# Attention output of one key group per matmul, and the projection weights loaded in two halves

## What is computed

```python
# 8 query heads of 64, 2 key/value heads: group g serves heads 4g .. 4g+3
qc = q.reshape(bsz, nc, CHUNK, N_KV_HEADS, rep, HEAD_DIM)          # nc = 4 chunks of 64 tokens, rep = 4
scores = jnp.einsum('bcqgrd,bckgd->bgrcqk', qc, kb) * (HEAD_DIM ** -0.5)   # kb: the chunk before and its own, 128 keys
probs = jax.nn.softmax(jnp.concatenate([scores, sink], axis=-1), axis=-1)[..., :WINDOW]
out = jnp.einsum('bgrcqk,bckgd->bcqgrd', probs, vb)
y_attn = out.reshape(bsz, s, ATTN_WIDTH) @ w_attn_o[l]              # 512 rows: head 4g+t, dim d -> row g*256 + t*64 + d
mixed = gate_a * y_attn + gate_c * y_conv + gate_s * y_ssm
```

## Time and profile before

| | us |
|---|---|
| median of 3 runs (951.61 to 953.21) | 951.86 |
| the profiled execution, its own time | 953.21 |
| its span, first to last instruction | 951.4 |
| PE busy, of the span | 909.5 |
| DVE busy | 709.5 |
| ACT busy | 480.5 |

### The profile page before, as it was taken

How to read it: one execution, slowest core, us unless ns; L and a number is a source line. 1 busy time by engine, 2 the same in 40 slices (tenths; PEclk the granted TensorE clock), 3 DMA queues, 4 the chain that set the end, 5 groups by cost and what they waited for, 6 DMA issues and landing times.

```text
span 951.4 us, 15656 instructions
## 1 busy us (share of the span) xinstructions
PE 909.5 (96%) x6575; PEld 767.0 (81%) x6575; DVE 709.5 (75%) x940; ACT 480.5 (51%) x600; POOL 19.9 (2%) x14
## 2 busy tenths in 40 slices
PE   5799999999999999999999999999999999999996
PEld 2598986767677989989997999777777888888885
DVE  3773998999667677866678487999967775666666
ACT  4574347732745566546336324684374544343434
POOL 2200000000000000000000000000000000000001
PEclk9899999999999999999999999999999999999998
DMA  8974365646886647876793924354878545655631
GB/s 355 253 229 135 134 210 189 232 136 253 288 284 210 238 150 242 311 250 221 243 328 96 266 90 134 133 163 147 290 265 313 195 157 190 207 177 181 199 107 45
DMA packets 128565, 196.10 MB, mean 206 GB/s; under 512 B 30729, under 2 KB 90641, under 8 KB 122351
## 3 DMA queue, kind: packets, MB, share of 16 engines
q1 hardware_dynamic: 126119, 194.89, 61.3%
q10 hardware_dynamic: 2376, 0.21, 0.2%
HBM read 194.02 MB, written 1.06 MB: 205 GB/s over the span
## 4 chain that ended last, share of the span: by engine, by line
PE 69%; DVE 19%; DMA 5%; issue 3%; ACT 2%; SPq 1%; POOL 1%; ACTq 0%; DVEq 0%
PE bank L614 16%; PE bank L616 15%; PE bank L615 15%; PE bank L980 8%; DVE wlo L1554 5%; DVE yc L1849 5%; PE bank L981 4%; DMA raw<-in_w_mod 3%; PE bank L652 2%; PE bank L718 2%; PE bank L847 1%; DMA uc<-in_ssm_c_im 1%; PE bank L900 1%; PE bank L742 1%; POOL uc L1132 1%
## 5 line engine op out<-in xcount | busy, mean ns | idle before, releaser
L1554 DVE TENSOR_TENSOR wlo<-raw,whi 128x2048 fp32r<-128x2048 f32 (+1 forms) x135 | 302.5, 2242 | 169.6 <-PE bank L616 86.0
L1171 ACT ACTIVATE whi<-raw 128x2048 fp32r<-128x2048 f32 x132 | 251.0, 1909 | 124.8 <-DMA raw<-in_w_in 57.3
L614 PE MATMUL bank<-hb,whi 128*128 128x256 f32 x592 | 170.9, 289 | 4.0 <-DVE wlo L1554 4.0
L616 PE MATMUL bank<-hb,wlo 128*128 128x256 f32 x592 | 168.1, 284 | 0.0
L615 PE MATMUL bank<-hb,whi 128*128 128x256 f32 x592 | 168.1, 284 | 0.0
L614 PE MATMUL bank<-whi,bhi 128*128 128x512 f32 x304 | 121.6, 400 | 2.1 <-DVE blo L1948 1.1
L614 PEld LDWEIGHTS bank<-hb,whi 128*128 128x128 f32 x592 | 114.1, 193 | 6.8 <-DVE wlo L1554 4.6
L980 PE MATMUL bank<-hb,whi 128*128 128x512 f32 x336 | 119.0, 398 | 0.0
L616 PE MATMUL bank<-whi,blo 128*128 128x512 f32 x304 | 118.7, 391 | 0.0
L615 PE MATMUL bank<-wlo,bhi 128*128 128x512 f32 x304 | 118.7, 390 | 0.0
L615 PEld LDWEIGHTS bank<-hb,whi 128*128 128x128 f32 x592 | 114.1, 193 | 0.4
(11 more groups left out here) (276 smaller groups left out, 1133.1 us busy)
## 6 DMA issues: line engine op xcount, KB each, us to landing
raw<-in_w_mod SPq DMA_DIRECT2D x48, 1024.0 KB, 6.2
raw<-in_w_ffn_in SPq DMA_DIRECT2D x44, 1024.0 KB, 5.1
raw<-in_w_in SPq DMA_DIRECT2D x38, 1024.0 KB, 6.9
raw<-in_w_ffn_out SPq DMA_DIRECT2D x22, 1024.0 KB, 5.0
raw<-in_w_out SPq DMA_DIRECT2D x8, 1024.0 KB, 7.6
raw<-in_w_in SPq DMA_DIRECT2D x16, 256.0 KB, 4.6
raw<-in_ssm_glu_b SPq DMA_DIRECT2D x4, 1024.0 KB, 6.2
raw<-in_ssm_glu_a SPq DMA_DIRECT2D x4, 1024.0 KB, 5.3
```

Of the source, the lines that this page charges most:

```text
L614: mm(o, w_hi, a_hi, start=start, stop=False, skip_group_check=True)
L616: return mm(o, w_lo, a_hi, start=False, stop=stop, skip_group_check=True)
L1171: fn(whi[mi % N_HI][:, :], raw[SLOT[item]][:, :], ACT.Copy).then_inc(s_hi, 1)
L1554: part = V.tensor_tensor(wlo[mi % N_LO][:, n], raw[SLOT[("main", *divmod(mi, NB))]][:, n], whi[mi % N_HI][:, n].bitcast(F32), ALU.subtract)
```

## The change

Each round of `attend` now puts its four heads side by side in the columns, on the 64 output partitions that belong to its key group: one matmul of 512 columns where two of 256 columns stood (j = 0), and two of 256 columns where four of 128 stood (j = 1). The copy `att_copy` covers 64 partitions by 512 columns, where it covered 128 by 256. `att[:, t, :]` then holds heads t and 4+t, so the rows of `w_attn_o` have to lie in that order too: each `ao` block is loaded by two transfers of 512 KB, one for each half of the partitions, and `N_LOADS` tells the wait that two transfers make one block. All other steps keep their places.

```diff
@@ -178,7 +178,7 @@
-N_LOADS = {"q": 4}
+N_LOADS = {"q": 4, "ao": 2}
...
@@ -537,8 +537,12 @@
-                if kind in ("ao", "cp", "gla", "glb"):
-                    w = A[{"ao": "w_attn_o", "cp": "conv_pw_w", "gla": "ssm_glu_a", "glb": "ssm_glu_b"}[kind]]
+                if kind == "ao":
+
+                    w = A["w_attn_o"][l].rearrange("(g t d) n -> g d t n", g=NKV, d=HEAD)
+                    return [(k4[g * HEAD:(g + 1) * HEAD], w[g][:, :, n * 512:(n + 1) * 512]) for g in range(NKV)]
+                if kind in ("cp", "gla", "glb"):
+                    w = A[{"cp": "conv_pw_w", "gla": "ssm_glu_a", "glb": "ssm_glu_b"}[kind]]
...
@@ -800,15 +804,13 @@
                 pe.wait_ge(pt_copied, n + 1)
-                for odd in range(2):
-                    o = b_t[odd * HEAD:(odd + 1) * HEAD, 0:2 * P].rearrange("p (t q) -> p t q", t=2)
-                    probs = pT[:, odd:4:2, :]
-                    if j == 0:
-                        last = mm(o, vv[:, 0, p], probs, start=True, stop=True, skip_group_check=True)
-                    else:
-                        for c in range(2):
-                            last = mm(o[:, :, c * CHUNK:(c + 1) * CHUNK], vv[:, 1 + c, p], probs[:, :, c * CHUNK:(c + 1) * CHUNK],
-                                      start=(c == 0), stop=(c == 1), skip_group_check=True)
+                o = b_t[p, :].rearrange("p (t q) -> p t q", t=4)
+                if j == 0:
+                    last = mm(o, vv[:, 0, p], pT[:, :, :], start=True, stop=True)
+                else:
+                    for c in range(2):
+                        last = mm(o[:, :, c * CHUNK:(c + 1) * CHUNK], vv[:, 1 + c, p], pT[:, :, c * CHUNK:(c + 1) * CHUNK],
+                                  start=(c == 0), stop=(c == 1), skip_group_check=True)
                 last.then_inc(pv_ready, 1)
...
@@ -1324,8 +1326,9 @@
                 j, g = divmod(r, 2)
+                p = slice(g * HEAD, (g + 1) * HEAD)
                 act.wait_ge(pv_ready, 4 * l + r + 1)
-                fn(att[:, 2 * g:2 * g + 2, j * P:(j + 1) * P], b_t[:, 0:2 * P].rearrange("p (t q) -> p t q", t=2), ACT.Copy).then_inc(at_copied, 1)
+                fn(att[p, :, j * P:(j + 1) * P], b_t[p, :].rearrange("p (t q) -> p t q", t=4), ACT.Copy).then_inc(at_copied, 1)
```

## The result

The changed kernel takes **954.09 us** (median of 20 runs, 947.47 to 956.98) against 948.00 us of the kernel before (20 runs, 942.70 to 953.21). The ratio is 1.0056, with a 95% interval of 1.0036 to 1.0077: it is slower by 0.6%. The profiled execution took 956.22 us with a span of 954.3; that of before had 953.21 and 951.4.

What follows compares the result with a forecast made beforehand. PE was taken as the bound (busy 909.5 of 951.4 us), nearly tied with DVE in layer 1's attention. Layer 0's 1.66 plus layer 1's 1.45, 3.1 us, on a median of 951.86 gave 955.0, range 953.1 to 957.2.

Steps and rivals of the forecast that it cites:

- The matmuls: Rounds of `attend` on PE: 0.42 us more for j = 0 and 0.41 for j = 1, old matmuls having overlapped.
- the rival without a price on PE: Rounds of `attend`: side-by-side streams share the feed at half rate, so new rounds cost the same; 952.1 us, chance 0.07.
- The Trainium skill's lower speed-up for tiles: Rounds of `attend`: by 2.38x for three tiles, an estimated 1.59x for two, round 0.92 us, whole sum 2.6 us.
- ACT's copy: `att_copy` on ACT: +0.21 us for each of eight, covered by idle time except ahead of scaling L1306 in layer 1.
- Layer 0: Layer 0's attention: four rounds before 189.2 us on a PE without idle time, paid in full, +1.66 us.
- Layer 1's attention: Layer 1's attention: 0.21 from the copy in the first round, then 0.42 and 2 x 0.41, +1.45 us.
- the rival in which layer 1 absorbs it: Layer 1: DVE's and ACT's chain hides PE's slip after the first round, paying only 0.21; 953.7 us, chance 0.14.
- The half loads: `ao` loads in two halves: 0.4 us delay from one more issue, costing nothing at layer 1's `mod` load.
- The bounds of 0 and 2.6: Delay of the `ao` half loads in us, bounded from quarter loads taken as 64 partitions; 2.6 would cost 0.6.
- the rival of late half loads: Layer 1's `mod` matmuls wait 3.1 us more because half-rate halves stretch the queue by 5.1; 958.1 us, chance 0.07.
- The room: Layer 1's `mod` load, landing 677.9, needed by PE at 678.46: 0.56 us to spare, 2.0 with PE 1.45 late.
- The base: Starting time of the kernel before: 951.86 us, the median of the runs shown, to which 3.1 us was added.

Runs made afterwards that it cites:

- that half alone: New attend and copy in layer 0 only, loads as before, against the kernel before: 950.63 us, ratio 1.0002; by group +1.3 and +1.7 us.
- the padded kernel: The changed kernel with 24 tiny unused transposes added on TensorE, making its program as long as before: 953.96 us, ratio 1.0081 against the kernel before.

## Why the prediction was right, and where not

The sign, the range and the place were right: slower, 954.09 in 953.1 to 957.2. The forecast of 955.0 was 0.9 us off, but that is luck, for two errors of 3 to 4 us stand against each other in it: the base stood 3.86 us too high, and the difference between the medians was 6.09, not 3.1. Of these 6.09, 4.35 to 4.95 is the change. The rest comes from the split: before has ten runs in each group and its median between them, the changed kernel nine and eleven.

- **The matmuls, right.** 0.42 and 0.41 a round were forecast, 0.42 and 0.42 measured, from L652 as the row with the same column count. That two streams on separate output columns had really run side by side, and that one alone isn't faster, was the step on which the sign hung; the rival without a price on PE is out.
- **The Trainium skill's lower speed-up for tiles, not borne out.** By its 2.38x for three tiles, in "TensorE: Matmul & The Clock Gate", section "Measured speedup vs the span model", the new round would have taken an estimated 0.92 us; it took 1.00. For two tiles of this shape the factor here is 1.00 / 0.58 = 1.7.
- **ACT's copy, right.** 0.21 forecast, 0.20 measured, paid once in layer 1.
- **Layer 0, right.** 1.66 forecast, 1.66 or 1.67 in every trace with the new matmuls, 1.3 and 1.7 in the times of that half alone.
- **Layer 1's attention, right.** 1.45 forecast, 1.43 to 1.49 measured, with the first round at 0.2: the rival in which layer 1 absorbs it is out.
- **The half loads, wrong, twice in the same direction.** The first wrong term was the delay: 0.4 us taken from one more issue, where 2.0 to 2.4 was measured (7.2 to 7.3 us for both halves instead of 4.9 to 5.2). The bounds of 0 and 2.6 held by luck, because the quarter loads of the earlier trace rows, from which the 2.6 comes, were misread. They don't go into 64 partitions: the kernel writes `k8[:, :, ...]`, all 128 partitions and 64 columns of each, and their packets are of 256 bytes (0.73 MB in 2879), where those of the half loads are of 2 KB. The DMA view of before over 513 to 516 us:

```profile
DMA packets 2879, 0.73 MB, mean 243 GB/s; under 512 B 2879, under 2 KB 2879, under 8 KB 2879
```

So they said nothing of 64 partitions, neither as a bound nor against the rival of late half loads, and no row of before did. The Trainium skill, "SBUF — State Buffer", section "Door 1", had given the right size, an estimate of 2.4 us.
- **The room, the more serious error.** The prediction gave the `mod` load 0.56 us of room, "and 2.0 with PE 1.45 late". But this load may be issued only when `lo` of `ao` 0 has freed its buffer, and that `lo` slips with PE as well. The load's issue and PE's need of it move together, so the room stays where it was: in every trace the need comes 12.4 to 12.5 us after `ao` 1's issue and the `mod` load's issue 5.37 us after it. With 0.56 and the bound of 2.6 the price would have been 2.0, not 0.6. Measured: 1.5.
- **The rival of late half loads** named the right place and the right sign (a wait of PE for `raw<-in_w_mod` behind 678), with a chance of 0.07 and a price of 3.1 from the same false room. It came true at half its size, 1.5 us beyond the other terms.
- **The base.** 951.86 was the median of three runs that all lay in the upper group; over 20 runs the base is 948.00. Against it the forecast of +3.1 would have been 951.1, and the measured difference is 4.35 to 4.95 by the cleaner comparisons. The record has 33 more runs of the changed kernel, without runs of before beside them: 24 of them lie at 952.54 or above, with a median of 955.29 for all. So how many runs fall into the upper group moves the median more than the change does. The profile of before held a hint: PE's 6.5 us wait for a copy on GpSimd of 7.05 us, where the same line takes 1.22 us in layer 1 (duration in ns, min/median/max of the two):

```profile
L1132 POOL COPY uc<-uc x2: 1221/4138/7055, 37.2 to 314.5; 128x512 f32<-128x512 f32 x2
```

## What to carry to other kernels

When a change makes two engines late, ask of every load behind it what releases its issue: room that seems to grow because the user is late is none if the release slips with the user. Take the cost of a transfer from a row that has the same partitions and the same packet size, and read both from the code and the packets; a row that is alike in bytes and pieces alone can come out near by chance. And when run times fall into two groups, compare two traces block by block before explaining anything else; here a single copy on one engine was worth more than the change under study.

## What the runs showed of the hardware

- **Half the partitions, 0.6 of the rate.** Loads into 64 partitions moved 225 GB/s with all DMA engines busy, those into 128 partitions 370, at the same 2 KB packets, and two queues in parallel didn't change it.
- **An instruction fetch is not free for a load.** One packet of 16 KB holds one DMA engine for 1.4 us here (4.5% of 16 engines in 2 us), 1.0 to 1.5 in the traces near this load. In the trace of before it lay in the `ao` 1 load of layer 1, which took 6.8 us (6.5 and 6.7 in two other traces with a fetch there), where the same load without one took 5.1 to 5.2 in three. The Trainium skill, "Runtime: NRT & Kernel Launch", section "Instruction fetch mechanics", calls the cost of crossing such a block mostly hidden; it says nothing there of the data that share the DMA engines with it, and for these the cost shows here. Queue q8 has 52 such packets in the trace of before, for some 13,000 instructions of TensorE (6575 matmuls and as many weight loads). The row of the 2 us around it, trace of before:

```profile
q8 instruction: 1, 0.02, 4.5%
```

- **The clock falls after short waits, not every time.** The granted clock went to 1.2 GHz behind the wait of 6.5 us in four traces of four, behind one of 2.1 us in layer 0's feed-forward part in eight of fourteen (1.3 us each time, and not in both traces of the same kernel), and behind the one of 1.9 us in the padded kernel, while waits of 1.9, 1.9 and 2.1 us near 57 us left it alone in three traces. A wait of about 2 us on a busy TensorE cost 2 us in some executions and 5 in one.
- **A copy on GpSimd of 0.7 to 1.0 or of 7.1 us, and VectorE beside it.** The long copies began before the short ones, the latest long one 4 ns before the earliest short one; that the start decides is not shown. What DVE does meanwhile fits in all twelve traces. From 36 or 37 us on it runs instructions with two tensors in SBUF without a pause, and near 44 us the first with one (`gate<-gate`). In the four traces with a long copy it ends 0.43 us after the start of this instruction, and the instruction takes 1.51 us; in all others it takes 1.23. Trace of before, and of the matmuls alone:

```profile
43.87 1.51 DVE L1649 TENSOR_TENSOR gate<-gate 128x1024 f32<-128x1024 f32 x1
...
44.34 1.23 DVE L1650 TENSOR_TENSOR gate<-gate 128x1024 f32<-128x1024 f32 x1
```

In the eight traces with a short copy one of DVE's `hb<-h,modv,hb` beside it takes 0.83 us instead of 0.48; in the four others and in the two with the copy on ScalarE none does. So the copy on GpSimd seems to find a place between two of DVE's instructions at once, or to stand until those with two tensors are over. The Trainium skill, "GPSIMD Engine Reference", section "Specifications", says that GpSimd shares its SBUF interfaces with VectorE and contends with such instructions; the traces agree. No run here took DVE's work away, so the cause is argued from this coincidence and not tested.
